# Inverse root of the norms between the stages: ScalarE's exponential of minus half the logarithm in place of its root and VectorE's reciprocal

## The reference, cut to what matters

```python
def rms_norm(x, w):
    xf = x.astype(jnp.float32)
    y = xf * lax.rsqrt(jnp.mean(xf * xf, axis=-1, keepdims=True) + EPS)   # EPS = 1e-6
    return (y * w.astype(jnp.float32)).astype(x.dtype)

def modulate(x, shift, scale):
    return x * (1 + scale) + shift

a_l = modulate(rms_norm(x, norm1_w[i]), mod_l[0], mod_l[1])   # before each stage
return rmsnorm(x, final_g)                                    # at the very end
```

## Time and profile before

| | |
|---|---|
| median of 3 runs | 2795.93 us (2793.19 to 2796.97) |
| the profiled execution | 2795.69 us, span 2793.8 us |
| TensorE busy | 2563.4 us, 92% of the span |
| VectorE busy | 1153.2 us, 41% |
| ScalarE busy | 649.0 us, 23% |
| mean granted TensorE clock | 0.973 of full speed |

### The profile page before, as it was taken

One profiled execution on the slowest core, in us unless ns is written; L12 is line 12 of the kernel. 1 busy time (PEld: TensorE's weight loads), 2 busy tenths in 40 slices (PEclk: granted clock), 3 DMA queues, 4 the chain that ended last, 5 costly groups with the idle time before them and its releaser, 6 DMA issues. The chain is left out here.

```text
span 2793.8 us, 32125 instructions
## 1 busy us (share of the span) xinstructions
PE 2563.4 (92%) x11820; PEld 1426.9 (51%) x11820; DVE 1153.2 (41%) x2538; ACT 649.0 (23%) x1251; POOL 28.4 (1%) x34
## 2 busy tenths in 40 slices
PE   7999999999999998999989899999989998777766
PEld 3555544444477777888554533333347774222322
DVE  4565777772245665871431522222243323111112
ACT  2342200000155553000242322222132222111111
POOL 0000000000000000000000000000010000000000
PEclk9999999999999999999999999999999999888888
DMA  8113555562322113884203799999953338999997
GB/s 342 78 61 116 194 232 233 232 256 75 120 76 76 63 59 113 306 306 175 91 16 121 305 411 421 421 422 421 422 210 136 135 116 362 421 422 422 422 422 302
DMA packets 104425, 665.87 MB, mean 238 GB/s; under 512 B 12617, under 2 KB 21065, under 8 KB 27664
## 3 DMA queue, kind: packets, MB, share of 16 engines
q1 hardware_dynamic: 99008, 652.30, 58.6%
q0 software_dynamic: 3600, 6.07, 0.6%
q10 hardware_dynamic: 1728, 6.29, 0.6%
HBM read 664.32 MB, written 7.34 MB: 240 GB/s over the span
## 5 line engine op out<-in xcount | busy, mean ns | idle before, releaser
L746 PE MATMUL PB<-A,RING 128*128 128x256 f32 (+1 forms) x1440 | 454.7, 479 | 2.9 <-DMA RING<-ffn_w 1.4
L746 PEld LDWEIGHTS PB<-A,RING 128*128 128x128 f32 x1440 | 273.3, 190 | 184.6 <-issue 160.4
L462 DVE SCALAR_TENSOR_TENSOR WORK<-RING,MORE 128x1024 f32<-128x1024 f32 x288 | 335.5, 1222 | 20.3 <-ACT MORE L760 11.8
L530 PE MATMUL PB<-BIG,RING 128*128 (+2 forms) x928 | 311.0, 497 | 6.1 <-PEq L709 3.3
L530 PEld LDWEIGHTS PB<-BIG,RING 128*128 128x128 f32 x928 | 175.8, 190 | 140.5 <-issue 129.9
L2630 DVE TENSOR_TENSOR BIG<-BIG,PB 64x512 f32<-64x512 f32 x32 | 22.1, 690 | 349.1 <-ACT BIG L2527 349.1
L3129 DVE TENSOR_TENSOR BIG<-BIG,PB 64x512 f32<-64x512 f32 x16 | 11.0, 690 | 372.8 <-ACT BIG L3047 372.8
L2947 PE MATMUL PB<-RING,X 128*32 128x512 f32 x384 | 106.5, 810 | 43.1 <-DMA RING<-moe_w 43.1
L622 DVE SCALAR_TENSOR_TENSOR X<-PB,MODS,X 128x256 f32<-128x256 f32 x72 | 32.5, 480 | 259.3 <-PE PB L559 258.5
L765 ACT ACTIVATE RS<-PB 128x512 f32<-128x512 f32 (+1 forms) x44 | 21.6, 491 | 414.8 <-PE PB L746 414.8
L575 ACT ACTIVATE WORK<-X 128x512 f32<-128x512 f32 (+1 forms) x36 | 20.2, 560 | 336.7 <-DVE X L622 336.7
(11 more groups left out here) (507 smaller groups left out, 3921.2 us busy)
## 6 DMA issues: line engine op xcount, KB each, us to landing
RING<-moe_w SPq DMA_DIRECT2D x144, 1024.0 KB, 25.2
RING<-ada_rows SPq DMA_DIRECT2D x80, 1024.0 KB, 6.8
RING<-ffn_w SPq DMA_DIRECT2D x66, 1024.0 KB, 4.8
SPARE<-moe_w SPq DMA_DIRECT2D x48, 1024.0 KB, 21.8
MORE<-moe_w SPq DMA_DIRECT2D x48, 1024.0 KB, 25.5
A<-moe_w SPq DMA_DIRECT2D x40, 1024.0 KB, 25.9
BIG<-moe_w SPq DMA_DIRECT2D x36, 1024.0 KB, 26.9
CST<-moe_w SPq DMA_DIRECT2D x24, 1024.0 KB, 23.3
```

What stands on the lines that cost most here:

```text
L462: dve_.scalar_tensor_tensor(out=JUNK[:, n % 4, :], in0=RING[:, s, b * D:(b + 1) * D], scalar=1.0, in1=WIDE[:, side // 2, w, :] if side els ...
L530: last = pe_.matmul(PB[:, m, 0:tp], tile(s, 2, D)[:, r, m * P:(m + 1) * P], src(2 * i + r), start=first and r == 0, stop=False)
L746: last = pe_.matmul(PB[:, 2 * s + j, x], tile(s, KD, P, j * KD * P)[:, k, :], A[:, k, x], start=k == 0, stop=k == KD - 1)
```

## The change

The root of the sum becomes a logarithm (of the mean square plus EPS), and ScalarE then takes the exponential of minus one half times it, in place, which gives the inverse root. VectorE's reciprocal goes. ScalarE waits for its own logarithm before the exponential, and signals `inverted` in VectorE's stead. The one-column activations ahead of the norms call the logarithm. The norms inside the mixers (lines 438, 1041, 1073, 1410, 2001) stay as they were.

```diff
@@ boundary
         def act_part(act):
             if product:
-                act_.activation(SMALL[:, 639:640], con("eps"), ACT.Sqrt)
+                act_.activation(SMALL[:, 639:640], con("eps"), ACT.Ln)
...
             for w in range(streams):
                 if product:
                     act.wait_ge(*of("summed", w + 1))
-                act_.activation(ROOT[:, 0, half(w)], PB[:, w if product else 0, half(w)], ACT.Sqrt, bias=con("eps"),
+                act_.activation(ROOT[:, 0, half(w)], PB[:, w if product else 0, half(w)], ACT.Ln, bias=con("eps"),
                                 scale=1.0 / D).then_inc(sig("rooted").sem, 1)
+                act.wait_ge(*of("rooted", w + 1))
+                act_.activation(ROOT[:, 0, half(w)], ROOT[:, 0, half(w)], ACT.Exp, scale=-0.5) \
+                    .then_inc(sig("inverted").sem, 1)
...
             for w in range(streams):
-                dve.wait_ge(*of("rooted", w + 1))
-                dve_.reciprocal(ROOT[:, 0, half(w)], ROOT[:, 0, half(w)]).then_inc(sig("inverted").sem, 1)
                 dve.wait_ge(*of("inverted", w + 1))
@@ final_norm
-                act_.activation(ROOT[:, 0, 0:S], PB[:, 0, 0:S], ACT.Sqrt, bias=con("eps"), scale=1.0 / D) \
+                act_.activation(ROOT[:, 0, 0:S], PB[:, 0, 0:S], ACT.Ln, bias=con("eps"), scale=1.0 / D) \
                     .then_inc(sig("rooted").sem, 1)
+                act.wait_ge(sig("rooted").sem, sig("rooted").at(1))
+                act_.activation(ROOT[:, 0, 0:S], ROOT[:, 0, 0:S], ACT.Exp, scale=-0.5).then_inc(sig("inverted").sem, 1)
...
-                dve.wait_ge(sig("rooted").sem, sig("rooted").at(1))
-                dve_.reciprocal(ROOT[:, 0, 0:S], ROOT[:, 0, 0:S]).then_inc(sig("inverted").sem, 1)
                 dve.wait_ge(sig("inverted").sem, sig("inverted").at(1))
```

## The result

The changed kernel takes 2815.98 us (median of 6 runs, 2810.13 to 2819.55) against 2794.43 (2793.19 to 2796.97): a ratio of 1.0077, 95% interval 1.0067 to 1.0087. It is 21.5 us slower. The forecast was slower by 8.0, with a range up to 2810: right in sign, much too small.

The account below looks back on a forecast made before the run. The prediction took the norm ahead of each stage to bound the kernel at the boundaries. Wait 6.5, one-stream norms -0.25 and clock 1.8 gave 8.0 us on the profiled 2795.69: 2803.7, range 2797 to 2810.

Parts of the forecast that it names:

- What bounds the kernel: The norm stands on the path in four of five two-stream boundaries, nearly so in the fifth, and at the end.
- One load for each change of function: On ScalarE, each switch between logarithm and exponential loads a table, 1.28 us; 83 loads in all.
- The first shift 2.70 later: At a two-stream boundary the first shift begins at 5.59 us instead of 2.89 after the root's or logarithm's start.
- One-stream norms nearly free: 0.1 to 0.15 us gained at the last router and the end, nothing at the second feed-forward layer; sum -0.25.
- Feed-forward and HGRN2 lose 1.2 each: After their two-stream boundaries these stages lose only 1.2 us each, 2.4 together, since TensorE waited for stream 1 before.
- the router and the odd mixer: After their two-stream boundaries the first router ends 1.0 us later and the odd mixer loses 0.4.
- The clock 1.8 us: Half clock after TensorE's longer stands: 0.9 us at the even mixer, 0.2 to 0.3 at the others and odd mixer.
- Rival 2: Loads are there, but later stages absorb the 1.2s and the clock holds: about +4 us, 2799.5; chance 0.20.
- Rival 3: The clock falls at every longer stand of TensorE, paid in full: 13 us slower, 2808.7; chance 0.15.
- Rival 1: One table serves logarithm and exponential, no load between them at the norms: 11.2 us faster, 2784.5; chance 0.08.

Follow-up runs that it names:

- the kernel kept at work: The changed kernel with four more products that nobody reads ahead of each two-stream boundary's reader; 2807.68 us, ratio 1.0050.
- the first experiment: The changed kernel with the table serving both logarithm and exponential loaded ahead of each norm's one-column logarithm; 2787.90 us, ratio 0.9976.
- one-stream norms alone: The changed kernel with root and reciprocal put back at the two-stream boundaries; 2795.31 us, ratio 1.0004.
- one boundary alone: The kernel before with unread one-column exponentials behind the roots only at the boundary into the even mixer; 2798.89 us, ratio 1.0016.
- grouped: The changed kernel with both streams' logarithms first and both exponentials behind them; 2793.73 us, ratio 0.9993.
- not kept at work: The kernel before without two of the products that nobody reads at each two-stream boundary; 2800.93 us, ratio 1.0019.
- loads alone: The kernel before, root and reciprocal kept, with an unread one-column exponential behind each root of the boundaries; 2813.43 us, ratio 1.0069.

## Why the prediction was wrong

Step by step:

- *What bounds the kernel*: right. The norm is on the path; a stretch that begins with a two-stream norm is longer, by what the first shift is late and by what the clock takes.
- *One load for each change of function*: right, at every place. 12 loads at exponentials, 5 at second logarithms, 83 in all as forecast (66 + 12 + 5 + 1 at the end + 1 after HGRN2 + 1 in the even mixer - 3 at the odd mixer and the routers). The logarithm took 0.473 us, the exponential 0.416, the load 1.283.
- *The first shift 2.70 later*: right, 2.73 in the trace. *One-stream norms nearly free*: right as far as the ratio of 1.0004 (0.9994 to 1.0013) can tell; the 0.25 us of gain is below what it can.
- *Feed-forward and HGRN2 lose 1.2 each*: wrong, this is the first step that failed. I read "47 in 10.38 us" as 0.22 us for one product. They are records, two to a product: the program has 16 products in the first router, and the trace of the kernel before counts 32 records for them:

```profile
L2347 PE MATMUL PB<-A,SMALL x32: 378/379/407, 1553.4 to 1561.5; 128*36 128x256 f32 x32
```

  A product of 256 columns takes 0.43 us, longer than a shift's 0.40. Stream 0's 16 products last 6.9 us, until 308.8, and stream 1's first shift was done at 306.7. TensorE never waited for stream 1, so there was no wait to be taken back: 2.7 carried in full, which is what the kernel kept at work shows (2.7 and 2.8). The same slip is in the router and the odd mixer. The router's 16 products take 6.9 us at full clock and without a pause after the change; before, TensorE paused 1.25 us for stream 1 between the first eight and the last. It ends 13.1 after the logarithm instead of 11.8. Worked again with 0.43, the wait is 3 x 2.7 + 1.3 + 0.9 = 10.3 us, not 6.5.
- *The clock 1.8 us*: wrong, and the larger miss. I took 3.4 us of half clock for each boundary and let the shifts' pace hide most of it. The same 0.22 made that cover: at half clock a product of 256 columns takes 0.86 us, not 0.43, twice the shifts' pace, so nothing is hidden. And in four boundaries of five the half clock lasted 6.8 to 6.9 us. The windows give 12.3 - 1.7 = 10.6 us, where 1.8 were forecast; the table of stretches leaves 22.4 - 10.3 = 12.1, of which 1.7 is the half clock at the odd mixer's end. Wait and windows together give 4.2, 5.1, 5.5, 4.2 and 1.9 for the five stretches, measured were 4.1, 5.2, 5.4, 4.1 and, with those 1.7 taken off, 1.9.
- *Rival 2* didn't happen: no two-stream boundary absorbed its delay whole. *Rival 3* had the right mechanism at 13 us, with the same wrong wait in it and 1.7 of clock at each boundary. With both terms put right the sum is 10.3 + 10.6 - 0.25 = 20.65, 2816.3 on the profiled 2795.69. The profiled execution of the changed kernel took 2818.68, the median is 2815.98. That the median is so near is in part luck, since half clock comes and goes elsewhere.
- *Rival 1*: as a mechanism of this program it didn't happen, but the first experiment made it happen. The Trainium skill ("ScalarE: Activation LUTs", section "Table sets: the hidden batching unit") lists a set that holds both functions, and the first experiment agrees that there is one: with set 6 loaded by hand, logarithm and exponential alternate without a load. The page's count of one load for a logarithm followed by an exponential doesn't hold for the changed kernel, which loads nothing by hand: at the boundaries 12 of 12 pairs had a load between. The rival's gain was forecast as 11.2 and measured as 7.2. The feed-forward layer's stretch is 1.0 shorter where 2.5 were forecast, by the same 0.22, and HGRN2's is as long as before (343.2 for 343.1) where 2.5 were forecast too: there TensorE starts 2.75 after the logarithm, when its weights are in, 0.8 sooner than before, and why that is lost again isn't shown.

Open: why half clock comes and goes away from the boundaries (ahead of the first norm, in the first experts, at the end of the odd mixer, and at the end of HGRN2, where the changed kernel has 6.8 us from 1063.9 for the 3.4 of before, at no cost that the table shows), whether the boundaries' lateness has a part in that, and the 1.0 and 1.1 of the one-stream stretches.

## What to carry to other kernels

Before alternating two functions on ScalarE, ask which table each load will fetch, not whether a table with both exists; then either load the common one by hand or put all of the one ahead of all of the other, which here turned 21.5 us lost into 7.2 gained or into nothing. A load costs what stands behind it on its engine: the three ahead of the shifts cost 0.9 to 2.7 us of wait and 1.0 to 2.9 us of clock at each boundary, the one in a one-stream norm cost nothing that could be measured. Before pacing an engine by its records, count the records against the program: here two made one product. The wrong wait came from that, the wrong clock from that and from half clock that lasted twice as long as assumed.

## What the runs showed of the hardware

How often half clock followed the stand of TensorE at the four two-stream boundaries with a product of their own, by the length of the stand, one profiled execution of each kernel:

| stand, us | kernel | half clock right after |
|---|---|---|
| 1.43 | before; one-stream norms alone; one boundary alone (its other three) | 0 of 11 |
| 1.80 | grouped | 0 of 4 |
| 3.14 | not kept at work | 1 of 4, 6.9 us |
| 3.71 | loads alone | 4 of 4: 3.4, 6.8, 3.4, 3.4 us |
| 3.71 | one boundary alone | 1 of 1: 3.4 us |
| 4.15 | changed | 4 of 4: 3.4, 6.9, 6.9, 6.8 us |

The half clock can begin while TensorE still stands (at the changed kernel's even mixer at 1354.0, where TensorE starts at 1355.3) or after it has started (with the loads alone at the first boundary at 303.3, where it starts at 302.6). I had not expected that after a stand of 4 us the 1.2 GHz level can last longer than the stand itself, while TensorE works without a break: the last 5.56 of 6.90 us at the even mixer. Four more products that nobody reads at each two-stream boundary, 0.9 us each while TensorE had nothing else to do (5.31 us for six), were worth 8.3 us in the changed kernel.
